# Attention: half of the outputs turned in mid-attention, outputs six items behind, and the output product begun on that half

## The chip, the core and the metric

One NeuronCore of a Trainium2 chip runs the whole program. The engines named here are TensorE (PE in the rows, its weight loads PEld), ScalarE (ACT), VectorE (DVE), GpSimd (POOL) and SyncE (SP, which issues the weight transfers). Each engine runs its own list of instructions in order, and they meet at semaphores. The metric is the device time of one execution in microseconds (us), lower is better. TensorE's clock is granted by the chip at one of two levels, 2.4 GHz (shown as 1.00) or 1.2 GHz (0.50).

## The reference, cut to what matters

256 tokens of width 1024 go through two stacks of two layers. Five attentions lie in them. In order: `x0` (cross attention of the first layer, 4 heads of 256), `dsa` (sparse attention on a shared latent, 8 heads of 128), `x1` (as `x0`), `mla` (16 heads: 8 causal latent and 8 dilated ones, 64 wide at the output) and `swa` (16 heads of 64, window and sinks). Each is scores, softmax, probabilities times values, and then a product with an output matrix that is added to the residual `h`:

```
def memory_cross_attn(h, mem_n, wq, wkv, wo):
    ...
    logits = jnp.einsum('bshd,bmhd->bhsm', q, k).astype(jnp.float32) * X_HEAD_DIM ** -0.5
    p = softmax32(logits, h.dtype)
    o = jnp.einsum('bhsm,bmhd->bshd', p, v).reshape(B_, S_, D_MODEL)
    return o @ wo
...
        h = h + memory_cross_attn(rmsnorm(h, xattn_norm[l]), mem_n, xattn_wq[l], xattn_wkv[l], xattn_wo[l])
        h = h + peer_ffn(rmsnorm(h, peer_norm[l]), peer_wq[l], peer_keys[l], peer_u[l], peer_v[l])
```

Behind every such product stands an RMS norm of `h`, which needs all of `h`. In `dsa` the heads' outputs first go through a per-head matrix `w_uv` (the groups `yc`), are put beside the output of a recurrent mixer, and then go through `odd_w_out`.

## The kernel before

**Numbers in halves.** All large products are made in three matmuls on rounded halves: left high by right high, high by low, low by high (`product`, L719 to L721). So every operand is split: ScalarE copies the high half (`wH` for weights at L495, `att_OTH` for attention outputs at L1201), and VectorE subtracts it to get the low half (`wL` at L505, `att_OTL` at L1577).

**Groups and banks.** TensorE's work is a fixed list of groups, written by `plan_groups`; each group fills one of the 8 PSUM banks, in turn, and has a reader, `act`, `dve` or `both` (ScalarE makes the high half from the bank, then VectorE the low one). A bank is used again only when its reader is done.

**Weights.** They come as a stream of blocks of 128 x 1024, two to a transfer, into `ring`; each block is split into one of 4 buffers (`NBUF`). Block b may be split once the group that reads block b - 4 last is done. Both splitting engines do this inside their own lists: `feed(eng, n)` is called ahead of each wait for group n, and puts there the splits of those blocks whose buffer is freed by a group ahead of n. So in an output product the split of block m + 4 stands in both lists between the residual adds of groups m and m + 1.

**An attention** (`attention`, in the program of each engine) walks over items, an item being a head and a half of the tokens (n = 8 items in `x0` and `x1`, 16 in `dsa`, 32 in `mla` and `swa`). At step i TensorE makes the scores S(i) (L803), turns the probabilities of item i - 2 (L816, `ATT_LAG_PT`), and multiplies those of item i - 5 with the values (L825, `ATT_LAG_O`). ScalarE makes the exponentials (L1255, L1261) and copies turned probabilities (L1270); VectorE makes maxima or logits (L1632, L1639, L1645) and scales the outputs into `att_O` (L1655, L1657). Ahead of the first turned item TensorE runs `spin`, matmuls without use.

When the last output is in `att_O`, TensorE turns `att_O` in 16 transposes into four banks (L834; token half `tt` by feature half `half`), ScalarE and VectorE make `att_OTH` and `att_OTL`, and TensorE waits for the last of these.

**The output product** (`lin`) is 8 groups, one for each 128 output features, each of 8 k by 3 matmuls. VectorE adds each group to `h` (`add`, L1613), ScalarE squares the sum for the norm (L1221), VectorE gathers squares (L1607). The norm's matmuls with ones are L740 and L742. `lin` has a second form, with `first`: then the first three groups (`LEAD`) go side by side, k by k, and `first(k)` waits for what k needs. It is used before where the input comes from a norm.

## Time and profile before

| | us |
|---|---|
| runs shown, median (lowest to highest) | 3050.76 (3049.41 to 3052.95) |
| the profiled execution, its own time | 3044.76 |
| its span, from the first to the last instruction | 3042.9 |
| TensorE matmuls busy | 2833.2 (93%) |
| VectorE busy | 1969.1 (65%) |
| ScalarE busy | 1463.9 (48%) |
| mean granted clock of TensorE | 0.964 |

The span is 1.9 us shorter than the profiled execution's own time, and that is 6.0 us below the median of the runs. Busy shares are means over stages of different kinds. An idle time in a timeline row stands in brackets at its end, with the engine and the instruction that ended it.

### The profile page before, as it was taken

The numbers are of one execution on the slowest core, as the hardware profiler recorded it, in microseconds if no ns is written. First come the engines' busy times: TensorE is split into PE (matmuls) and PEld (weight loads), VectorE is DVE, ScalarE is ACT, GpSimd is POOL, SyncE is SP. The second block draws the span as 40 slices with busy tenths as digits, with TensorE's granted clock in tenths as the row PEclk, the third lists the DMA queues.
The fourth block names the chain that finished last, engine by engine and source line by source line (L and its number), as shares of the span: only waits on it lengthen the run. The fifth ranks groups of instructions, "written<-read, shape, count | busy, mean of one in ns | idle before, by whom it ended". The sixth has DMA issues, their size and how long they took to land.

```text
span 3042.9 us, 57274 instructions
## 1 busy us (share of the span) xinstructions
PE 2833.2 (93%) x19570; PEld 2641.4 (87%) x19570; DVE 1969.1 (65%) x4218; ACT 1463.9 (48%) x2414; POOL 345.1 (11%) x199
## 2 busy tenths in 40 slices
PE   7889889999999998878899999999999789999998
PEld 6878789999988887868898999988888679998998
DVE  5544961887466666685589688557776566555555
ACT  4444344444455554454444444445555454445443
POOL 0002686000000000000069200000000000000000
PEclk8999999999999998889999999999999899999999
DMA  3434455445666664323245554666666324551454
GB/s 151 166 139 144 158 189 207 173 172 173 232 243 241 240 241 170 134 84 139 111 170 193 187 173 175 211 242 241 241 241 231 132 84 156 187 225 70 165 182 166
DMA packets 140449, 546.16 MB, mean 179 GB/s; under 512 B 15784, under 2 KB 81592, under 8 KB 83616
## 3 DMA queue, kind: packets, MB, share of 16 engines
q1 hardware_dynamic: 63216, 455.38, 41.7%
q10 hardware_dynamic: 73728, 67.14, 6.9%
q0 software_dynamic: 3376, 21.88, 1.9%
q8 instruction: 85, 1.39, 0.2%
q14 instruction: 44, 0.36, 0.0%
HBM read 505.53 MB, written 40.91 MB: 180 GB/s over the span
## 4 chain that ended last, share of the span: by engine, by line
PE 75%; DVE 8%; DMA 6%; POOL 4%; ACT 4%; issue 3%; ACTq 0%; SPq 0%; DVEq 0%
PE bank L719 22%; PE bank L720 21%; PE bank L721 21%; POOL wL L505 4%; PE bank L907 4%; DMA ring<-in_w_stream 3%; ACT wH L495 3%; DMA act_parked<-act_out 3%; DVE wL L505 2%; PE bank L803 1%; PE bank L825 1%; PE bank L816 1%; DVE act_out L1589 1%; PE bank L790 1%; DVE h L1613 1%
## 5 line engine op out<-in xcount | busy, mean ns | idle before, releaser
L505 DVE TENSOR_TENSOR wL<-ring,wH 128x1024 fp32r<-128x1024 f32 x744 | 909.2, 1225 | 769.9 <-ACT wH L495 769.1
L719 PE MATMUL bank<-hnH,wH 128*128 128x256 f32 x3648 | 1062.3, 291 | 60.8 <-DVE hnL L1571 31.0
L495 ACT ACTIVATE wH<-ring 128x1024 fp32r<-128x1024 f32 x864 | 909.3, 1055 | 341.8 <-DMA ring<-in_w_stream 160.9
L720 PE MATMUL bank<-hnL,wH 128*128 128x256 f32 x3648 | 1044.5, 286 | 0.0
L721 PE MATMUL bank<-hnH,wL 128*128 128x256 f32 x3648 | 1043.9, 286 | 0.0
L719 PEld LDWEIGHTS bank<-hnH,wH 128*128 128x128 f32 x3648 | 712.6, 195 | 72.3 <-issue 43.8
L720 PEld LDWEIGHTS bank<-hnL,wH 128*128 128x128 f32 x3648 | 713.3, 196 | 0.1
L721 PEld LDWEIGHTS bank<-hnH,wL 128*128 128x128 f32 x3648 | 711.8, 195 | 0.0
L719 PE MATMUL bank<-wH,wgtH 128*128 128x512 f32 x1024 | 399.4, 390 | 4.6 <-issue 4.5
L720 PE MATMUL bank<-wL,wgtH 128*128 128x512 f32 x1024 | 398.9, 390 | 0.0
L721 PE MATMUL bank<-wH,wgtL 128*128 128x512 f32 x1024 | 398.8, 389 | 0.0
L505 POOL TENSOR_TENSOR wL<-ring,wH 128x1024 fp32r<-128x1024 f32 x120 | 315.5, 2649 | 123.0 <-ACT wH L495 97.3
L1321 ACT ACTIVATE act_out<-bank 128x256 f32<-128x256 f32 x256 | 97.8, 382 | 393.9 <-PE bank L721 333.7
L719 PEld LDWEIGHTS bank<-wH,wgtH 128*128 128x128 f32 x1024 | 192.6, 188 | 45.4 <-issue 5.4
L1345 ACT ACTIVATE wgtH<-gates 128x256 fp32r (+1 forms) x256 | 107.0, 418 | 256.3 <-PE bank L721 255.9
L721 PEld LDWEIGHTS bank<-wH,wgtL 128*128 128x128 f32 x1024 | 192.5, 188 | 40.1
L720 PEld LDWEIGHTS bank<-wL,wgtH 128*128 128x128 f32 x1024 | 192.6, 188 | 39.9
L1741 DVE TENSOR_SCALAR onehot<-con,slotT 128x128 f32<-128x128 f32 x512 | 174.1, 340 | 0.0
L1740 DVE TENSOR_SCALAR onehot<-con,slotT 128x128 f32<-128x128 f32 x512 | 143.2, 280 | 18.7 <-ACT slotT L1360 18.7
L907 PE MATMUL bank<-onehot 128*128 128x128 f32 x1024 | 136.9, 277 | 9.1 <-DVE onehot L1741 9.1
L907 PEld LDWEIGHTS bank<-onehot 128*128 128x128 f32 x1024 | 127.0, 193 | 9.5 <-DVE onehot L1741 9.5
L1754 DVE TENSOR_TENSOR wgtL<-gates,wgtH 128x256 fp32r<-128x256 f32 x256 | 107.5, 420 | 12.8 <-ACT wgtH L1345 12.3
(347 smaller groups left out, 3398.3 us busy)
## 6 DMA issues: line engine op xcount, KB each, us to landing
ring<-in_w_stream SPq DMA_DIRECT2D x432, 1024.0 KB, 4.9
act_parked<-act_out ACTq DMA_DIRECT2D x256, 128.0 KB, 3.6
act_in<-act_parked ACTq DMA_DIRECT2D x256, 128.0 KB, 2.7
sw_bias<-in_c_swa POOLq DMA_DIRECT2D x1, 4096.0 KB, 14.6
relb_rows<-rel_table POOLq DMA_DIRECT2D x1, 2048.0 KB, 9.3
h_parked<-h POOLq DMA_DIRECT2D x2, 1024.0 KB, 6.3
h_back<-h_parked POOLq DMA_DIRECT2D x2, 1024.0 KB, 6.3
od_relb<-relb_rows POOLq DMA_DIRECT2D x2, 1024.0 KB, 8.1
```

Source lines behind the costliest of these rows:

```text
L495: eng.activation(wH[:, b % NBUF, :], raw(b), ACT.Copy).then_inc(w_high, 1)
L505: eng.tensor_tensor(wL[:, b % NBUF, :], raw(b), wH[:, b % NBUF, :].bitcast(F32), ALU.subtract).then_inc(w_low, 1)
L719: pe.matmul(dst, lh, rh, start=start, stop=False, skip_group_check=True)
L720: pe.matmul(dst, lh, rl, start=False, stop=False, skip_group_check=True)
L721: return pe.matmul(dst, ll, rh, start=False, stop=stop, skip_group_check=True)
L790: pe.matmul(psum[bank_of[n]][:, :], wH[:, b % NBUF, 0:P], wH[:, b % NBUF, 0:512], start=True, stop=True)
L907: last = pe.matmul(psacc[j][:, m * P:(m + 1) * P], onehot[:, k, :], onehot[:, 8 + k, :], start=True, stop=True)
L1321: act.activation(act_out[:, c % 2, :], psum[c % BANKS][:, 0:T], ACT.Gelu_apprx_tanh).then_inc(u_read, 1)
L1345: act.activation(wgtH[:, c % 2, :].unsqueeze(1), gates[:, bass.ds(i * 4 + c, 1), :], ACT.Copy).then_inc(wgt_high, 1)
L1740: dve.tensor_scalar(onehot[:, k, :], iota, slotT[:, 2, bass.ds(tok, 1)], None, ALU.is_equal)
L1741: last = dve.tensor_scalar(onehot[:, 8 + k, :], iota, slotT[:, 1, bass.ds(tok, 1)], slotT[:, 0, bass.ds(tok, 1)], ALU.is_equal, ALU.mult)
L1754: dve.tensor_tensor(wgtL[:, c % 2, :].unsqueeze(1), gates[:, bass.ds(i * 4 + c, 1), :], wgtH[:, c % 2, :].bitcast(F32).unsqueeze(1), ALU.s ...
```

## The change

Four things are changed, for all five attentions.

1. The lags are 3 (turned probabilities) and 6 (outputs), in place of 2 and 5, on all engines.
2. The four turned banks are no longer made at the end. Feature half 0 (two banks, 8 transposes) is turned behind step n/2 - 1 + 8, two steps after the last item of the first half of the heads has its output; half 1 at the end. ScalarE and VectorE make the halves at the same places of their lists.
3. The output products `x0o`, `x1o`, `e_out` and `o_out` use the form with three groups side by side; k = 0 waits for half 0, k = 4 for half 1.
4. In `dsa`, `yc` 0 and 1 wait for half 0 only, `yc` 2 and 3 for half 1; `odd_out` has three groups side by side, takes k = 4 to 7 first (the recurrent mixer's output), then k = 0 to 3, each behind its `yc`.

```
-ATT_LAG_PT, ATT_LAG_O = 2, 5
+ATT_LAG_PT, ATT_LAG_O = 3, 6
+ATT_LAG_OT = ATT_LAG_O + 2
...
+            def turned(kind):
+                return lambda k: read_of(pe, (kind, "OT", NT - 1, k // 4)) if k % 4 == 0 else None
...
-            def lin(name, ms, src, nk=DC, per=1, width=P, rows=T, first=None):
+            def lin(name, ms, src, nk=DC, per=1, width=P, rows=T, first=None, parts=None):
...
+                parts = list(parts or range(nk))
...
-                for k in range(nk if lead else 0):
+                for k in parts if lead else []:
...
+                def turn_outputs(half, j):
+                    read_of(pe, (kind, "O", j))
+                    for tt in range(NT):
+                        ps = bank((kind, "OT", tt, half))
+                        for c in range(4):
+                            cc = half * 4 + c
+                            last = pe.transpose(ps[:, c * P:(c + 1) * P], att_O[:, tt, cc * P:(cc + 1) * P], ident)
+                        last.then_inc(group_done, 1)
...
+                    if i - ATT_LAG_OT == len(items) // 2 - 1:
+                        turn_outputs(0, len(items) // 2 - 1)
+                turn_outputs(1, len(items) - 1)
...
-                read_of(pe, (x, "OT", NT - 1, 1))
-                lin(x + "o", range(8), (att_OTH, att_OTL))
+                lin(x + "o", range(8), (att_OTH, att_OTL), first=turned(x))
...
-            read_of(pe, ("dsa", "OT", NT - 1, 1))
             for j in range(4):
                 ps = bank(("yc", j))
+                if j % 2 == 0:
+                    read_of(pe, ("dsa", "OT", NT - 1, j // 2))
...
-            read_of(pe, ("yc", 3))
             pe.wait_ge(hg_y, 4)
-            lin("odd_out", range(8), (od_yH, od_yL))
+            lin("odd_out", range(8), (od_yH, od_yL), first=lambda k: read_of(pe, ("yc", k)) if k < 4 else None,
+                parts=(4, 5, 6, 7, 0, 1, 2, 3))
...
+                def halves_of(half):
+                    for tt in range(NT):
+                        high_of((kind, "OT", tt, half), att_OTH[:, half * 4:half * 4 + 4, tt * P:(tt + 1) * P],
+                                src=lambda ps: ps[:, :].rearrange("p (a b) -> p a b", a=4))
...
+                    if i - ATT_LAG_OT == len(items) // 2 - 1:
+                        halves_of(0)
+                halves_of(1)
```

VectorE has the same `halves_of` with `low_of`, and `e_out` and `o_out` are called as `x0o` is.

**TensorE at the end of `x0`.** Before, the last outputs (`att_PT` by `x_v`) and then the transposes of `att_O`:

```order
L825 MATMUL bank2<-x_v,att_PT 128x256 [waits read_by_act]
L825 MATMUL bank2<-x_v,att_PT 128x256
L825 MATMUL bank3<-x_v,att_PT 128x256 [waits read_by_act]
L825 MATMUL bank3<-x_v,att_PT 128x256
L834 MATMUL bank4<-con,att_O 128x128 [waits read_by_dve]
L834 MATMUL bank4<-con,att_O 128x128 x3
L834 MATMUL bank5<-con,att_O 128x128 [waits read_by_act]
L834 MATMUL bank5<-con,att_O 128x128 x3
L834 MATMUL bank6<-con,att_O 128x128 [waits read_by_dve]
```

The same place after:

```order
L844 MATMUL bank1<-x_v,att_PT 128x256 [waits read_by_act]
L844 MATMUL bank1<-x_v,att_PT 128x256
L812 MATMUL bank2<-con,att_O 128x128 [waits read_by_dve]
L812 MATMUL bank2<-con,att_O 128x128 x3
L812 MATMUL bank3<-con,att_O 128x128 [waits read_by_act]
L812 MATMUL bank3<-con,att_O 128x128 x3
L844 MATMUL bank4<-x_v,att_PT 128x256 [waits read_by_act,read_by_dve]
L844 MATMUL bank4<-x_v,att_PT 128x256
L844 MATMUL bank5<-x_v,att_PT 128x256 [waits read_by_act]
L844 MATMUL bank5<-x_v,att_PT 128x256
L812 MATMUL bank6<-con,att_O 128x128 [waits read_by_dve]
L812 MATMUL bank6<-con,att_O 128x128 x3
```

Half of the transposes now stand two outputs ahead of the end.

**TensorE at the start of `x0o`**, before and then after:

```order
L719 MATMUL bank<-att_OTH,wH 128x256 [waits w_low,read_by_dve]
L720 MATMUL bank<-att_OTL,wH 128x256
L721 MATMUL bank<-att_OTH,wL 128x256
L719 MATMUL bank<-att_OTH,wH 128x256
L720 MATMUL bank<-att_OTL,wH 128x256
```

```order
L722 MATMUL bank0<-att_OTH,wH 128x256 [waits w_low,read_by_dve]
L723 MATMUL bank0<-att_OTL,wH 128x256
L724 MATMUL bank0<-att_OTH,wL 128x256
L722 MATMUL bank1<-att_OTH,wH 128x256 [waits w_low]
L723 MATMUL bank1<-att_OTL,wH 128x256
L724 MATMUL bank1<-att_OTH,wL 128x256
L722 MATMUL bank2<-att_OTH,wH 128x256 [waits w_low]
L723 MATMUL bank2<-att_OTL,wH 128x256
```

The first matmuls went one after another to one group's bank, and now go to three groups in turn.

**VectorE from the last low halves of `x0` into `x0o`**, before and then after (`h` is the residual add, `wL` the low half of a weight block):

```order
L1577 TENSOR_TENSOR att_OTL<-bank,att_OTH 128x4x128 [waits bank_high,group_done] x4
L1613 TENSOR_TENSOR h<-h,bank 128x256 [waits group_done]
L505 TENSOR_TENSOR wL<-ring,wH 128x1024 [waits w_high]
L1613 TENSOR_TENSOR h<-h,bank 128x256 [waits group_done]
L505 TENSOR_TENSOR wL<-ring,wH 128x1024 [waits w_high]
L1613 TENSOR_TENSOR h<-h,bank 128x256 [waits group_done]
```

```order
L1595 TENSOR_TENSOR att_OTL<-bank,att_OTH 128x4x128 [waits bank_high,group_done] x2
L1631 TENSOR_TENSOR h<-h,bank 128x256 [waits group_done]
L508 TENSOR_TENSOR wL<-ring,wH 128x1024 [waits w_high]
L1631 TENSOR_TENSOR h<-h,bank 128x256 [waits group_done]
L508 TENSOR_TENSOR wL<-ring,wH 128x1024 [waits w_high]
L1631 TENSOR_TENSOR h<-h,bank 128x256 [waits group_done]
```

Two of the four low halves went away from here; behind them the order is the same in both.

## Rows read from the trace of the kernel before

**Rows 1.** The page, part 4: the chain that ended last, by engine.

```profile
PE 75%; DVE 8%; DMA 6%; POOL 4%; ACT 4%; issue 3%; ACTq 0%; SPq 0%; DVEq 0%
```

**Rows 2.** Timeline, TensorE, end of `x0`: start, duration (us), instruction, [idle before].

```profile
223.96 1.97 PE L834 MATMUL bank<-con,att_O 128*128 128x128 f32 x16 [0.65 <-DVE att_O L1657]
227.89 0.53 PE L719 MATMUL bank<-att_OTH,wH 128*128 128x256 f32 x1 [1.97 <-DVE att_OTL L1577]
```

**Rows 3.** Timeline, ScalarE and VectorE, the same stretch and the first add.

```profile
224.65 1.57 ACT L1201 ACTIVATE att_OTH<-bank 128x512 fp32r<-128x512 f32 x3 [4.38 <-PE bank L834]
...
225.35 1.29 DVE L1577 TENSOR_TENSOR att_OTL<-bank,att_OTH 128x512 fp32r<-128x512 f32 x2 [1.45 <-ACT att_OTH L1201]
...
232.55 0.42 DVE L1613 TENSOR_TENSOR h<-h,bank 128x256 f32<-128x256 f32 x1 [4.71 <-PE bank L721]
```

**Rows 4.** Timeline, VectorE and ScalarE in `e_out`: adds, and a block's split.

```profile
2502.36 0.42 DVE L1613 TENSOR_TENSOR h<-h,bank 128x256 f32<-128x256 f32 x1 [3.19 <-PE bank L721]
2504.22 1.23 DVE L505 TENSOR_TENSOR wL<-ring,wH 128x1024 fp32r<-128x1024 f32 x1 [1.44 <-ACT wH L495]
2505.36 0.41 DVE L1613 TENSOR_TENSOR h<-h,bank 128x256 f32<-128x256 f32 x1
...
2523.30 0.41 DVE L1613 TENSOR_TENSOR h<-h,bank 128x256 f32<-128x256 f32 x1
...
2503.14 1.04 ACT L495 ACTIVATE wH<-ring 128x1024 fp32r<-128x1024 f32 x1
```

**Rows 5.** Timeline, TensorE from the end of `mla` through `e_out` to the norm.

```profile
2495.30 1.97 PE L834 MATMUL bank<-con,att_O 128*128 128x128 f32 x16 [0.56 <-DVE att_O L1657]
2499.23 0.39 PE L719 MATMUL bank<-att_OTH,wH 128*128 128x256 f32 x1 [1.97 <-DVE att_OTL L1577]
...
2521.84 0.28 PE L721 MATMUL bank<-att_OTH,wL 128*128 128x256 f32 x1
2524.20 0.67 PE L740 MATMUL bank<-sq,con 128*128 128x256 f32 x2 [2.08 <-DVE sq L1607]
2524.71 0.61 PE L742 MATMUL bank<-sq,con 128*128 128x256 f32 x2
```

**Rows 6.** Timeline, end of `swa`: the transposes and the first add of `o_out`.

```profile
2803.19 0.99 PE L834 MATMUL bank<-con,att_O 128*128 128x128 f32 x7 [0.56 <-DVE att_O L1657]
...
2811.60 0.42 DVE L1613 TENSOR_TENSOR h<-h,bank 128x256 f32<-128x256 f32 x1 [4.53 <-PE bank L721]
```

**Rows 7.** Windows: stretch, length, busy PE, PEld, DVE, ACT, POOL; clock; DMA.

```profile
228.00:231.40 3.40, 3.40 (x16) 3.40 (x17) 0.00 (x0) 0.22 (x2) 0.00 (x0) 0.50 0.00 0
...
2463.00:2495.30 32.30, 31.17 (x206) 25.11 (x204) 22.07 (x126) 22.86 (x96) 0.00 (x0) 1.00 0.02 6
...
2529.00:2535.40 6.40, 6.21 (x29) 6.24 (x30) 6.07 (x15) 3.74 (x8) 0.00 (x0) 0.50 0.01 3
```

**Rows 8.** Timeline, TensorE: the norm's passes where the clock was low.

```profile
1192.34 1.19 PE L740 MATMUL bank<-sq,con 128*128 128x256 f32 x2 [2.40 <-DVE sq L1607]
1193.33 1.06 PE L742 MATMUL bank<-sq,con 128*128 128x256 f32 x2
```

**Rows 9.** Timeline, TensorE: waits for probabilities in `mla` (two) and `swa`.

```profile
2465.43 0.30 PE L816 MATMUL bank<-con,att_P 128*128 128x128 f32 x1 [0.26 <-ACT att_P L1261]
...
2493.04 0.30 PE L816 MATMUL bank<-con,att_P 128*128 128x128 f32 x1 [0.31 <-ACT att_P L1261]
...
2800.94 0.30 PE L816 MATMUL bank<-con,att_P 128*128 128x128 f32 x1 [0.37 <-ACT att_P L1261]
```

**Rows 10.** Timeline, `dsa`: the fourth logits, the last exponential, transposes, first add.

```profile
1360.40 0.43 DVE L1639 SCALAR_TENSOR_TENSOR att_L<-bank,od_relb 128x256 f32<-128x256 f32 x1 [0.52 <-PE bank L803]
...
1374.02 0.51 ACT L1261 ACTIVATE att_P<-att_L,small 128x256 f32<-128x256 f32 x1 [0.61 <-DVE small L1645]
...
1377.28 0.33 PE L834 MATMUL bank<-con,att_O 128*128 128x128 f32 x1 [0.77 <-DVE att_O L1657]
...
1389.96 0.42 DVE L1613 TENSOR_TENSOR h<-h,bank 128x256 f32<-128x256 f32 x1
```

More of the change, by code:

```diff
@@ L116, in att @@
                 g((kind, "O", i - ATT_LAG_O), "dve")
+            if i - ATT_LAG_OT == len(items) // 2 - 1:
+                for tt in range(NT):
+                    g((kind, "OT", tt, 0), "both")
         for tt in range(NT):
-            for half in range(2):
-                g((kind, "OT", tt, half), "both")
+            g((kind, "OT", tt, 1), "both")
     def norm(name):
@@ L827, in attention @@
                         last.then_inc(group_done, 1)
-                read_of(pe, (kind, "O", len(items) - 1))
-                for tt in range(NT):
-                    for half in range(2):
-                        ps = bank((kind, "OT", tt, half))
-                        for c in range(4):
-                            cc = half * 4 + c
-                            last = pe.transpose(ps[:, c * P:(c + 1) * P], att_O[:, tt, cc * P:(cc + 1) * P], ident)
-                        last.then_inc(group_done, 1)
+                    if i - ATT_LAG_OT == len(items) // 2 - 1:
+                        turn_outputs(0, len(items) // 2 - 1)
+                turn_outputs(1, len(items) - 1)
             def keys_values(l):
@@ L1141, in _ @@
                       lambda hd, s: (ml_vA if hd < 8 else ml_vB)[:, s, (hd % 8) * 64:(hd % 8 + 1) * 64])
-            read_of(pe, ("mla", "OT", NT - 1, 1))
-            lin("e_out", range(8), (att_OTH, att_OTL))
+            lin("e_out", range(8), (att_OTH, att_OTL), first=turned("mla"))
             ffn(0)
@@ L1152, in _ @@
                       lambda hd, s: sw_v[:, s, (hd // 8) * 64:(hd // 8 + 1) * 64])
-            read_of(pe, ("swa", "OT", NT - 1, 1))
-            lin("o_out", range(8), (att_OTH, att_OTL))
+            lin("o_out", range(8), (att_OTH, att_OTL), first=turned("swa"))
             ffn(1)
@@ L1235, in attention @@
                 base = att_base[kind]
+                def halves_of(half):
+                    for tt in range(NT):
+                        high_of((kind, "OT", tt, half), att_OTH[:, half * 4:half * 4 + 4, tt * P:(tt + 1) * P],
+                                src=lambda ps: ps[:, :].rearrange("p (a b) -> p a b", a=4))
                 act.activation(small[:, 82:83], eps, ACT.Exp)
@@ L1270, in attention @@
                         act.activation(att_PT[:, j % DEEP, 0:span], ps[:, 0:span], ACT.Copy).then_inc(read_by["act"], 1)
-                for tt in range(NT):
-                    for half in range(2):
-                        high_of((kind, "OT", tt, half), att_OTH[:, half * 4:half * 4 + 4, tt * P:(tt + 1) * P],
-                                src=lambda ps: ps[:, :].rearrange("p (a b) -> p a b", a=4))
+                    if i - ATT_LAG_OT == len(items) // 2 - 1:
+                        halves_of(0)
+                halves_of(1)
             def cross(l):
@@ L1619, in attention, with halves_of @@
                 hv = ATT_V[kind]
+                def halves_of(half):
+                    for tt in range(NT):
+                        place = (FULL, slice(half * 4, half * 4 + 4), slice(tt * P, (tt + 1) * P))
+                        low_of((kind, "OT", tt, half), att_OTL[place], att_OTH[place],
+                               src=lambda ps: ps[:, :].rearrange("p (a b) -> p a b", a=4))
                 for i in range(len(items) + ATT_LAG_O):
@@ L1658, in attention @@
                                           ALU.mult).then_inc(read_by["dve"], 1)
-                for tt in range(NT):
-                    for half in range(2):
-                        place = (FULL, slice(half * 4, half * 4 + 4), slice(tt * P, (tt + 1) * P))
-                        low_of((kind, "OT", tt, half), att_OTL[place], att_OTH[place],
-                               src=lambda ps: ps[:, :].rearrange("p (a b) -> p a b", a=4))
+                    if i - ATT_LAG_OT == len(items) // 2 - 1:
+                        halves_of(0)
+                halves_of(1)
             def peer(l):
```

4 lines of the change are left out of this document (2 added, 2 removed).

## The prediction

> **What bounds the kernel now.** I read the page's chain of work that ended last first: TensorE holds 75% of it [rows 1], so an edit pays only where TensorE stands still or where it takes work off TensorE. The five attentions are short stretches, so I then read the timelines of TensorE, ScalarE and VectorE around the end of each.
>
> There is a hole there. After the last head's output TensorE waits 0.65 us for VectorE, turns the outputs in 16 transposes (1.97 us) and stands another 1.97 us until the halves are made [rows 2]. ScalarE starts on the first turned bank 0.69 us after TensorE started, VectorE 0.70 us after that, and two of VectorE's low halves take 1.29 us [rows 3]. The same 1.97 us stands ahead of `e_out` [rows 5]. This is what the change is after.
>
> What ends the stage is something else. The stage behind the hole is the output product (`x0o`, `x1o`, `e_out`, `o_out`, `odd_out`): eight groups of 24 matmuls, (2521.84 - 2499.23)/191 = 0.118 us apart, so 2.84 us a group [rows 5]. Beside it VectorE adds each group to `h`. In `e_out` the first add starts at 2502.36, the second at 2505.36, the eighth at 2523.30 [rows 4]: (2523.30 - 2502.36)/7 = 2.99 us apart, longer than a group. The rows between show a closed loop: add (2502.36), ScalarE's square of it, ScalarE's split of the next weight block (2503.14, 1.04 us), VectorE's low half of it (2504.22, 1.23 us), next add (2505.36) [rows 4]. Each engine runs its list in order, and between two adds stands one block in both lists, so after the first add the loop sets the pace, however early TensorE has its groups. TensorE ends its last product at 2521.84 and stands 2.08 us for the norm, released by VectorE, whose eighth add starts at 2523.30 [rows 4, 5]. **The end of an output product is therefore the start of its first add plus 20.94 us**, and the change is to be priced at the first add.
>
> **The change, part by part.** Let T be the start of the transposes that stand behind the last head.
>
> *The end of the attention.* Before, first add - T is 232.55 - 223.96 = 8.59 us in `x0` [rows 2, 3] (1471.34 - 1462.75, the same, in `x1`, whose rows repeat these), 2502.36 - 2495.30 = 7.06 in `mla` [rows 4, 5] and 2811.60 - 2803.19 = 8.41 in `swa` [rows 6]. The extra 1.5 us in three of them is the clock: TensorE was granted 0.50 from 228.0 to 231.4, at the start of `x0o` [rows 7], that is 1.2 GHz in place of 2.4.
>
> After, 8 transposes stand there (0.98 us) and the product begins at once, on half 0. Half 1 is ready at T + 0.69 + 0.70 + 1.29 = T + 2.68, while the first four k of three groups keep TensorE until T + 0.98 + 36 x 0.118 = T + 5.2: the 1.97 us wait is hidden. But the product now begins with three groups side by side. Group 0 no longer ends after 24 matmuls but after 66 (72 less the last two groups' three each): 66 x 0.118 = 7.79 us. The first add follows the end of its group by 2502.36 - 2499.23 - 24 x 0.118 = 0.30 us [rows 4, 5]. So first add - T becomes 0.98 + 7.79 + 0.30 = 9.07 us at full clock. That is +0.48 in `x0` and `x1`, +2.01 in `mla`, +0.66 in `swa`. The three groups that are then ready together do not help: their adds still come 2.99 us apart. The weights come in time: block 4 is ready at the second add, first add + 3.0, and group 0 freed it 0.7 us before the lead's end, so it is there 2.5 us behind the lead, while group 3 keeps TensorE 2.84 us.
>
> *Turning half 0 in mid-attention.* In `x0`, `x1`, `mla` and `swa` TensorE has next to no idle time in mid-attention (31.17 of 32.30 us busy in `mla`) [rows 7], so the moved 8 transposes cost their 0.98 us there. VectorE's two low halves (1.24 us and a wait for ScalarE) come behind the output of item n/2 + 1. In `mla` and `swa` six or more items follow and the deeper lag covers it (I take 0, at most 0.5 each). In `x0` and `x1` only two outputs follow, so the last output comes about 0.40 us later: VectorE is done with half 0 1.7 us after TensorE left the transposes, and two outputs of 0.6 us each follow, to 2.9, where before it would have been 2.5.
>
> *Lags 3 and 6.* TensorE's waits for probabilities go: 0.26 at the start and 0.31 at the end of `mla`, 0.37 at the end of `swa` [rows 9]. In `x0` and `x1` there are none to win. The counts of matmuls stay.
>
> *The sparse attention `dsa`* is bound by VectorE. The fourth item's wait goes (0.52) [rows 10], and the last output that VectorE does ahead of the last logits is one less (0.46). But half 0 now stands behind the last logits: ScalarE does a 0.51 us exponential [rows 10] and the accumulator read, a copy and the first high half (about 1.65 in all, an estimate from the durations here and in rows 3) while VectorE does one output (0.5), so it stands 1.15 us and then works 1.24. Before, its waits there were 0.54 less one output, and the sum is +1.5 us at T (1377.28) [rows 10]. From T on: half 1 at 2.7 us, 12 matmuls of `yc` 1.42, then 7.79 + 0.30, so 12.25 us against 1389.96 - 1377.28 = 12.68 [rows 10]. In sum +1.05. The wait ahead of `odd_out` is gone, and the lead eats it.
>
> *The norm behind.* TensorE now ends its product at T + 0.98 + 22.7 and gets the norm at T + 9.07 + 20.94 + 0.9: it stands 7.2 us where it stood 2.08. The norm's four passes took 1.12 us (2524.20 to 2525.32) [rows 5] and, at another place where the granted clock was at the low level, 2.05 us (1192.34 to 1194.39) [rows 8]: +0.93, taken for four; half of it for `dsa`. In sum 4.2. The product behind the norm began at clock 0.50 already [rows 7], so nothing is added there. The bounds are 0 and 4.7.
>
> **Sum.** `x0` and `x1`: 0.48 + 0.98 + 0.40 = 1.86 each. `mla`: 2.01 + 0.98 - 0.57 = 2.42. `swa`: 0.66 + 0.98 - 0.37 = 1.27. `dsa`: 1.05. Together 8.5, and 4.2 for the norms: **+12.7 us**. The profiled execution took 3044.76 us (span 3042.9), the median of the runs is 3050.76, 6.0 above it; I carry the same distance: 3044.76 + 12.7 + 6.0 = 3063.4.
>
> The trace shows the low clock at the start of `x0o` after a stretch in which TensorE stood 0.65, worked 1.97 and stood 1.97 us [rows 2, 7]. The Trainium skill, page "TensorE: Matmul & The Clock Gate", section on HAM oscillation, advises arranging work so that TensorE does not stand between bursts, since it then starts the next one at half clock; the trace agrees for this hole. By the page alone the edit closes five holes and should win. By the rows it closes them and opens longer ones at the end of the same products, ahead of the norm.
>
> **Rivals.** *The gain arrives* (the other side: faster). The adds would follow TensorE, if the loop had slack: one period under 2.84 us would do, and it is 2.99. The last add would then follow T by 0.98 + 8 x 2.84 + 0.3 = 24.0 us. Before it was 8.59 + 20.94 = 29.5 in `x0` and `x1`, 28.0 in `mla`, 29.35 in `swa`; with the other terms that is -4.1, -4.1, -3.4 and -4.8, about -5 in `dsa`: -21 us, 3029. Against it: the lists of ScalarE and VectorE at the adds are unchanged, and the period is 2.99 in all five. That the loop decides only in part, and a smaller loss or none remains, is the middle case: 3048 to 3057.
>
> *The clock falls in the lead.* If TensorE gets the low level for 3.4 us at the start of the product as it does now [rows 7], the first add comes 1.6 us later in up to five places: up to +8, 3067 to 3072. For it: a wait of some 0.6 to 1.0 us stays ahead of T. Against: the 1.97 us wait goes.
>
> *The norm stays at full clock:* 8.5 us, 3059, within the forecast's own range.
>
> *The turning doesn't hide:* half 1 would have to be later than T + 5.2; from T + 2.68 that is far, and I give it nothing.
>
> **How the numbers follow.** Forecast and norm case, 3057.5 to 3067: 0.66. Low clock in the leads, 3067 to 3072: 0.15. Middle case: 0.13, nearly all of it within 0.2%. The gain arrives: 0.06. A measurement of this kernel can tell about 0.2%, 6.1 us, from no change. Slower by more: 0.66 + 0.15 and 0.01 of the middle, 0.82; the same 0.12; faster 0.06. The range of 8 in 10 is 3055 to 3070: it leaves out the gain, most of the middle case and the top of the low-clock case.
>
> **What the profile after would show.** Right: in `e_out` the first add 9.1 us behind the last transposes' start, adds 2.99 us apart, TensorE idle some 7 us ahead of the norm and its passes near 1.0 us instead of 0.5; no wait of 1.97 us behind the transposes; no wait for probabilities in `mla` and `swa`; first add - T near 9.07 in four attentions. Wrong: adds closer than 2.84 us apart (then the gain arrives), a first add 10.5 us behind T (the low clock), or a wait of TensorE in mid-attention behind half 0 of `mla` and `swa` (then the lag of six is too small).

## The result, and the profile of the changed kernel

| | before | after |
|---|---|---|
| median of the runs, us (lowest to highest) | 3050.84 (3045.64 to 3058.17, 20 runs) | 3060.96 (3047.29 to 3077.25, 20 runs) |
| ratio, 95% interval | | 1.0035 (1.0025 to 1.0046) |
| span of the profiled execution, us | 3042.9 | 3055.2 |
| mean granted clock | 0.964 | 0.959 |

The interval lies above 1: the changed kernel is slower, by some 0.35%. The ratio is worth 0.0035 x 3050.84 = +10.7 us; the spans differ by 12.3 us. The forecast was +12.7 us, 3063.4, with slower by more than 0.2% as the likeliest sign.

The page of after, part 4, answers to [rows 1]: the chain of work is TensorE's as before.

```profile
PE 76%; DVE 7%; DMA 6%; ACT 4%; POOL 4%; issue 3%; ACTq 0%; SPq 0%; DVEq 0%
```

**The hole is gone.** TensorE's timeline of after at the end of `x0` (start, duration in us, instruction, idle before it in brackets) answers to [rows 2]: two times eight transposes, and the product's first matmul directly behind the second eight.

```profile
220.06 1.04 PE L812 MATMUL bank<-con,att_O 128*128 128x128 f32 x8
...
223.92 1.09 PE L812 MATMUL bank<-con,att_O 128*128 128x128 f32 x8 [1.09 <-DVE att_O L1683]
224.77 0.36 PE L722 MATMUL bank<-att_OTH,wH 128*128 128x256 f32 x1
```

The waits for probabilities went as well. The view of TensorE's waits in after, over the whole of `mla` (2468.0 to 2504.4), has two rows, and the waits of [rows 9] are in neither:

```profile
PE bank L798 <- ACT ml_vA L1243: 1.1, 1, 1.1
PE bank L812 <- DVE att_O L1683: 0.6, 1, 0.6
```

**And a longer wait is there.** VectorE and ScalarE in `e_out` of after, against [rows 4]. The low halves of the outputs are done at 2505.78 + 1.29 = 2507.07. Then VectorE stands 6.22 us for the end of the first group:

```profile
2505.78 1.29 DVE L1595 TENSOR_TENSOR att_OTL<-bank,att_OTH 128x512 fp32r<-128x512 f32 x2 [1.45 <-ACT att_OTH L1213]
2513.29 0.42 DVE L1631 TENSOR_TENSOR h<-h,bank 128x256 f32<-128x256 f32 x1 [6.22 <-PE bank L724]
2515.15 1.23 DVE L508 TENSOR_TENSOR wL<-ring,wH 128x1024 fp32r<-128x1024 f32 x1 [1.43 <-ACT wH L498]
2516.29 0.42 DVE L1631 TENSOR_TENSOR h<-h,bank 128x256 f32<-128x256 f32 x1
...
2534.23 0.42 DVE L1631 TENSOR_TENSOR h<-h,bank 128x256 f32<-128x256 f32 x1
...
2513.75 0.42 ACT L1233 ACTIVATE sq<-h 128x256 f32<-128x256 f32 x1 [6.06 <-DVE h L1631]
2514.07 1.04 ACT L498 ACTIVATE wH<-ring 128x1024 fp32r<-128x1024 f32 x1
```

The order add, square, high half, low half, add is as before, and the adds are (2534.23 - 2513.29)/7 = 2.99 us apart. TensorE, which had its groups early, pays behind them: 6.56 us of standing where [rows 5] have 2.08, and passes of the norm at the price of [rows 8], 1.19 + 1.06 in place of 0.67 + 0.61. Its timeline in `mla` and behind `e_out`:

```profile
2468.03 1.66 PE L798 MATMUL bank<-wH 128*128 128x512 f32 x6 [1.10 <-ACT ml_vA L1243]
...
2504.39 1.09 PE L812 MATMUL bank<-con,att_O 128*128 128x128 f32 x8 [0.56 <-DVE att_O L1683]
...
2535.12 1.19 PE L747 MATMUL bank<-sq,con 128*128 128x256 f32 x2 [6.56 <-DVE sq L1625]
2536.11 1.06 PE L749 MATMUL bank<-sq,con 128*128 128x256 f32 x2
2541.04 0.55 PE L722 MATMUL bank<-hnH,wH 128*128 128x256 f32 x1 [3.87 <-DVE hnL L1589]
```

The windows of after (stretch, length, busy time of the engines, granted clock, DMA share, GB/s) answer to [rows 7]. The first stretch is the start of `x0o`, at full clock where it was at half; the second the end of the transposes of `dsa`, still low; the third the wait and the norm behind `e_out`.

```profile
223.90:233.00 9.10, 9.08 (x78) 9.08 (x79) 1.47 (x3) 2.58 (x4) 0.00 (x0) 1.00 0.01 2
...
1383.10:1387.00 3.90, 3.88 (x20) 3.89 (x21) 1.78 (x3) 1.58 (x3) 1.10 (x2) 0.56 0.12 25
2533.80:2541.00 7.20, 2.04 (x4) 1.17 (x4) 4.34 (x8) 1.87 (x5) 0.00 (x0) 0.50 0.39 146
```

**Where the time went.** Take an attention from its first matmul without use (`spin`) to the first matmul behind the norm that follows it. In `mla` of after that is 2541.04 - 2468.03 = 73.01 us. The same two rows of before:

```profile
2458.80 1.66 PE L790 MATMUL bank<-wH 128*128 128x512 f32 x6 [1.10 <-ACT ml_vA L1231]
...
2529.19 0.55 PE L719 MATMUL bank<-hnH,wH 128*128 128x256 f32 x1 [3.87 <-DVE hnL L1571]
```

give 70.39, so +2.62. The five in the order of the program grew by 2.49 (`x0`), 2.26 (`dsa`), 2.53 (`x1`), 2.62 (`mla`) and 1.31 us (`swa`), together +11.2 of the 12.3 us. The other 1.1 us lie in stretches that the change does not touch; more on these below.

### The profile page after: what moved, and what is told of

Read it like the earlier page. It is cut to its first block, busy times and chain, and to the rows that moved or that the text cites. A ratio compares the mean times of both kernels' runs of the same rounds, so it can differ in the third digit from the quotient of the medians.

```text
span 3055.2 us, 57274 instructions
## 1 busy us (share of the span) xinstructions
PE 2836.1 (93%) x19570; PEld 2642.0 (86%) x19570; DVE 1969.1 (64%) x4218; ACT 1465.6 (48%) x2414; POOL 345.0 (11%) x199
## 4 chain that ended last, share of the span: by engine, by line
PE 76%; DVE 7%; DMA 6%; ACT 4%; POOL 4%; issue 3%; ACTq 0%; SPq 0%; DVEq 0%
PE bank L722 22%; PE bank L723 22%; PE bank L724 22%; PE bank L920 4%; POOL wL L508 4%; DMA act_parked<-act_out 3%; ACT wH L498 3%; DMA ring<-in_w_stream 2%; PE bank L822 2%; DVE wL L508 1%; PE bank L844 1%; PE bank L835 1%; DVE act_out L1607 1%; PE bank L798 1%; DVE h L1631 1%
## 5 line engine op out<-in xcount | busy, mean ns | idle before, releaser
L1778 DVE TENSOR_TENSOR wgtL<-gates,wgtH 128x256 fp32r<-128x256 f32 x256 | 107.8, 421 | 12.5 <-ACT wgtH L1363 11.9
```

Source lines behind the costliest of these rows:

```text
L1778: dve.tensor_tensor(wgtL[:, c % 2, :].unsqueeze(1), gates[:, bass.ds(i * 4 + c, 1), :], wgtH[:, c % 2, :].bitcast(F32).unsqueeze(1), ALU.s ...
```

## The experiments

In all of them T is the start of the (last) transposes behind the last head, and "the attentions" is the sum of the five stretches just defined: 320.0 us in the kernel before, 331.2 in the kernel after.

### One group at the start, in place of three

```
-            def lin(..., first=None, parts=None):
+            def lin(..., first=None, parts=None, ahead=LEAD):
...
-                lead = ms[0:LEAD] if first is not None else []
+                lead = ms[0:ahead] if first is not None else []
...
-                lin(x + "o", range(8), (att_OTH, att_OTL), first=turned(x))
+                lin(x + "o", range(8), (att_OTH, att_OTL), first=turned(x), ahead=1)
```

and `ahead=1` for the other four output products.

> The kernel after, but the five output products begin with one group on half 0 (12 matmuls, then the wait for half 1) in place of three side by side. Loop theory (end of product = first add + 20.94 us, and the lead of three delays the first add): first add at T + 2.68 + 12 x 0.118 + 0.30 = T + 4.4 us where it is T + 8.9 in the kernel after, so -4.5 us in x0, x1, mla and swa, 42 matmuls less ahead of the first add of odd_out, -5.0; together -23, and up to -4.6 more if the norms return to the full clock: 3033 to 3038 us, faster than the kernel before. Rival (the loss comes from the turning in mid-attention, the lags or the norm's clock, and the lead has no part in it): within 3 us of the kernel after, 3058 to 3064.

3043.32 us, ratio to the kernel before 0.9972 (0.9960 to 0.9985). VectorE in `e_out`, T = 2494.98:

```profile
2499.44 0.42 DVE L1631 TENSOR_TENSOR h<-h,bank 128x256 f32<-128x256 f32 x1 [1.78 <-PE bank L724]
2502.43 0.42 DVE L1631 TENSOR_TENSOR h<-h,bank 128x256 f32<-128x256 f32 x1
...
2520.38 0.41 DVE L1631 TENSOR_TENSOR h<-h,bank 128x256 f32<-128x256 f32 x1
```

The first add stands at T + 4.46 (4.40 to 4.46 in the four, 4.4 expected), the others follow 2.99 us apart, the eighth at the first + 20.94. The attentions take 306.9 us, 24.3 less than in the kernel after. So the three groups side by side are what makes the changed kernel slower: with one group the same change is a gain. The median came out 5 us above the expectation's upper end, and not in the attentions, whose 24.3 us lie within the expected 23 to 27.6.

### The plain product behind the new turning

The wait for both halves and the plain `lin` of the kernel before are put back, the rest of the change stays:

```
-                lin(x + "o", range(8), (att_OTH, att_OTL), first=turned(x))
+                read_of(pe, (x, "OT", NT - 1, 1))
+                lin(x + "o", range(8), (att_OTH, att_OTL))
```

> The kernel after, but the five output products have the form and the wait of the kernel before (both halves waited for, eight groups one after another). Turning in mid-attention and the lags stay. Loop theory: first add at T + 2.68 + 2.84 + 0.30 = T + 5.8, -3.1 us in four attentions against the kernel after, about -5 in dsa, together -17, and up to -4.6 for the norms: 3039 to 3044. It would then be faster than the kernel before, and the lead would be the whole of the loss. Rival (turning in mid-attention and the lags cost more than the shorter end gives): 3051 or more.

3045.16 us, ratio 0.9989 (0.9978 to 1.0000). The first add was at T + 5.88 in `swa`, as expected, but at T + 7.37 to 7.39 in `x0`, `x1` and `mla`: TensorE stood 1.64 us for the halves ahead of `x0o` again, and from 229.5 to 232.5 its granted clock was 0.53, as in [rows 7]. The attentions took 315.6 us. The time is 1 us above the expected 3039 to 3044, and its interval ends at 1: a gain over the kernel before is not shown, one over the kernel after (1.0035) is.

Read beside the run with the lags alone (below), it prices the turning in mid-attention. T comes 6.5 us later in the sum of the five than with the lags alone (1.3 in `x0` and `x1`, 2.2 in `dsa`, 0.9 in `mla` and `swa`), and the first add is 1.2 us nearer to T where the clock at the start of the product is the same (5.88 against 7.07 in `swa`, 7.37 against 8.59 in `x1`), about 6 us in the five. With a plain product behind it the early turning therefore brings nothing; what it makes possible is a product that begins on half 0.

### Three groups side by side alone

```
-                lin(x + "o", range(8), (att_OTH, att_OTL))
+                lin(x + "o", range(8), (att_OTH, att_OTL), first=lambda k: None)
```

and so for the other four; nothing else of the change.

> The kernel before, but the five output products have three groups side by side, after the same wait for both halves; nothing is turned early and the lags are 2 and 5. Loop theory: first add 42 matmuls later, 42 x 0.118 = 4.96 us, and the norm waits so much longer: +3.4 us (where the clock at the start of the product comes back to full) to +5.0 in each of five, +17 to +25, and +0.9 for each norm that falls to the low clock, at most 4.6: 3068 to 3080. Rival (the adds catch up with the three ready groups): the last add follows TensorE, no change, 3049 to 3053.

3084.44 us, ratio 1.0113 (1.0098 to 1.0127). VectorE in `x0o`, T = 223.91:

```profile
235.92 0.42 DVE L1613 TENSOR_TENSOR h<-h,bank 128x256 f32<-128x256 f32 x1 [8.13 <-PE bank L721]
...
256.85 0.41 DVE L1613 TENSOR_TENSOR h<-h,bank 128x256 f32<-128x256 f32 x1
```

The first add is at T + 12.01 in all four, from 1.97 + 1.97 + 7.79 + 0.30 = 12.03. Against the kernel before the first adds come 3.42 (`x0`, `x1`), 4.94 (`dsa`), 4.95 (`mla`) and 3.60 us (`swa`) later, 20.3 in sum, and with 4.3 for the norms and 0.2 ahead of T in `dsa` the attentions grew by 24.8 us to 344.8, as expected (17 to 25, and at most 4.6 for the norms). The time is 4.4 us above the expected 3068 to 3080; the two stretches that no edit touches, of which more below, were 8.8 and 8.7 us longer than in the trace of before. The rival, that the adds catch up with three finished groups, is out: (256.85 - 235.92)/7 = 2.99 us apart here too.

### Opening the loop

ScalarE makes the split ahead of its wait for the add:

```
-                        added(act, adds or order[order.index(name) - 1], c)
+                        last = adds or order[order.index(name) - 1]
+                        if ADDS.get(last) in ("x0o", "odd_out", "x1o", "e_out", "o_out"):
+                            feed(act, NO[(ADDS[last], c)] + 1)
+                        added(act, last, c)
```

> The kernel after, but in the five output products ScalarE splits the high half of the next weight block ahead of its wait for the add, not behind its square of the sum; the same instructions otherwise. Loop theory: the loop is open, the adds catch up with TensorE, the eighth follows T by 0.98 + 8 x 2.84 + 0.3 = 24.0 us in place of 29.8: -5.8 us in four, about -5 in dsa, and 0 to -4.6 for the norms: 3028 to 3033. Adds behind the first three groups 2.84 us apart, the first ones 2.1 to 2.6. Rival (the pace of 2.99 us is the engines' own work, not the order): adds stay 2.99 us apart and the time within 3 us of the kernel after.

3033.84 us, ratio 0.9950 (0.9934 to 0.9966): 27 us below the kernel after, by moving one instruction of each step in ScalarE's list. VectorE, ScalarE and, in the last row, TensorE in `x0o`, T = 226.49:

```profile
235.39 0.42 DVE L1634 TENSOR_TENSOR h<-h,bank 128x256 f32<-128x256 f32 x1 [6.22 <-PE bank L724]
237.69 0.41 DVE L1634 TENSOR_TENSOR h<-h,bank 128x256 f32<-128x256 f32 x1
239.15 0.41 DVE L1634 TENSOR_TENSOR h<-h,bank 128x256 f32<-128x256 f32 x1
...
240.95 0.42 DVE L1634 TENSOR_TENSOR h<-h,bank 128x256 f32<-128x256 f32 x1
...
245.02 1.23 DVE L508 TENSOR_TENSOR wL<-ring,wH 128x1024 fp32r<-128x1024 f32 x1 [3.32 <-ACT wH L498]
246.16 0.42 DVE L1634 TENSOR_TENSOR h<-h,bank 128x256 f32<-128x256 f32 x1
...
235.45 1.06 ACT L498 ACTIVATE wH<-ring 128x1024 fp32r<-128x1024 f32 x1 [5.67 <-PE bank L724]
...
243.93 1.06 ACT L498 ACTIVATE wH<-ring 128x1024 fp32r<-128x1024 f32 x1 [3.91 <-DMA ring<-in_w_stream]
...
254.48 1.22 PE L749 MATMUL bank<-sq,con 128*128 128x256 f32 x2 [1.34 <-ACT sq L1236]
```

The split starts at 235.45, 0.06 us behind the start of the add where it was 0.78 in the kernel after, and the adds come 2.30 and 1.46 us apart: the 2.99 us were the order and not the work. The first add is still at T + 8.91. The next limit shows at once: with the splits made this early, ScalarE waits 3.91 us for the transfer of a weight block, and the fifth add comes 5.2 us behind the fourth. The eighth add is at T + 25.1 in `x0`, late by this wait, and at T + 23.7 in `x1`, where 24.0 was expected and TensorE's last group sets it.

This edit stands at all eight groups, and it has a price of its own: at the eighth group ScalarE's square, for which the norm waits, now stands behind the split of a block that is still on its way. In `x0`, `mla` and `swa` the norm's second pair of matmuls waits 1.34, 1.18 and 1.34 us for that square, and the next product begins 7.1 to 7.2 us behind the start of the norm, in `dsa` and `x1` 5.1.

### The same edit in the kernel before

The same lines, for groups 0 to 6 only (`c < DC - 1`), so that the last square stays ahead of the split behind it.

> The kernel before, but in the five output products ScalarE splits the next weight block ahead of its wait for the add (for groups 0 to 6), as in the run of the kernel after with the same edit. Loop theory: the pitch of the adds falls from 2.99 us to TensorE's 2.84, so the eighth add comes 7 x 0.15 = 1.05 us earlier in each of five: -5 us, 3045 to 3047. With the kernel after and the same edit at 3034, the change itself would then be worth about -11 us once the loop is open. Rival (the pace is the engines' own work): 2.99 stays, 3050.

VectorE in `x0o`:

```profile
233.22 0.42 DVE L1616 TENSOR_TENSOR h<-h,bank 128x256 f32<-128x256 f32 x1 [4.71 <-PE bank L721]
...
236.04 0.42 DVE L1616 TENSOR_TENSOR h<-h,bank 128x256 f32<-128x256 f32 x1 [0.45 <-PE bank L721]
...
253.00 0.42 DVE L1616 TENSOR_TENSOR h<-h,bank 128x256 f32<-128x256 f32 x1 [0.45 <-PE bank L721]
```

Seven steps take 19.78 us, 2.83 each, and every add now waits for TensorE. The norm follows 0.94 us behind the product where it was 2.08. The attentions fell by 8.9 us to 311.1: 5.8 for the loop (20.94 to 19.78 in each of the five), most of the rest because `x1o` and `o_out` began at full clock here (first adds at T + 7.06 and 7.07, where the kernel before has 8.59 and 8.41). But the time did not fall: 3049.47 us, ratio 1.0001 (0.9991 to 1.0010), where 3045 to 3047 was expected.

**Where did 9 us go?** In the two profiled executions, into code that no kernel here edits. From the end of `x0` to `dsa` (258.9 to 1365.3) and from the end of `x1` to `mla` (1504.5 to 2470.5), the windows of before, then of this kernel:

```profile
259.40:1354.20 1094.80, 1028.55 (x6860) 952.21 (x6860) 734.88 (x1638) 524.73 (x798) 187.19 (x91) 0.96 0.54 190
1498.20:2458.80 960.60, 919.48 (x6122) 849.19 (x6122) 685.38 (x1541) 472.07 (x719) 144.66 (x56) 0.98 0.57 201
```

```profile
258.90:1365.30 1106.40, 1040.07 (x6860) 962.55 (x6860) 735.18 (x1638) 524.90 (x798) 187.08 (x91) 0.95 0.54 187
1504.50:2470.50 966.00, 924.79 (x6123) 854.68 (x6123) 686.14 (x1541) 472.64 (x719) 144.50 (x56) 0.97 0.57 200
```

The same 6860 matmuls keep TensorE busy 11.5 us longer, at a clock of 0.95 in place of 0.96, and the second stretch is 5.4 us longer. The place can be seen: some 28 and 62 us behind the end of the attention `x0`. TensorE's timeline of before has a wait of 1.00 us,

```profile
286.37 0.33 PE L719 MATMUL bank<-wH,pr_qH 128*128 128x128 f32 x1 [1.00 <-DVE pr_qL L1577]
```

and that of this kernel the same,

```profile
285.11 0.33 PE L719 MATMUL bank<-wH,pr_qH 128*128 128x128 f32 x1 [1.00 <-DVE pr_qL L1580]
```

and two windows behind it read, before and then in this kernel:

```profile
288.00:296.00 8.00, 8.00 (x71) 8.00 (x71) 0.43 (x1) 4.39 (x7) 4.50 (x2) 1.00 0.30 123
322.00:330.00 8.00, 8.00 (x69) 8.00 (x68) 7.79 (x51) 3.60 (x6) 5.84 (x4) 1.00 0.20 80
```

```profile
288.00:296.00 8.00, 8.00 (x39) 8.00 (x39) 0.00 (x0) 2.74 (x4) 1.44 (x2) 0.50 0.22 92
322.00:330.00 8.00, 8.00 (x39) 8.00 (x39) 7.79 (x50) 2.22 (x5) 0.30 (x1) 0.50 0.37 132
```

Behind the same wait of 1.00 us, and with TensorE busy for 8.00 of 8.00 us, one kernel is granted 2.4 GHz and does 71 matmuls, the other 1.2 GHz and 39. By these counts 10 us at the low level do the work of 5.5 at the high one: each such stretch costs about 4.5 us, an estimate.

The two stretches together are 16.9 us longer here, more than the 9 us that were to be explained. That is because a profile shows one execution: the one of the kernel before took 6.1 us less than the median of its runs, the one of this kernel 3.2 us more. By the ratio, which no single execution decides, the code outside the attentions takes some 9 us more in this kernel.

### Matmuls without use ahead of the norm

```
             def rms(name):
                 i = NORM_NO[name]
+                if name in ("peer0", "x1", "peer1", "ffn0", "ffn1"):
+                    spin(26)
```

> The kernel after, with 26 matmuls without use (0.21 us each at full clock, 5.5 us) on TensorE ahead of the five norms behind the output products, where it stands 6.6 us. If the low clock of the norm comes from this idle time: the passes take 1.1 us again in place of 2.05, -4 to -5 us over five, and the product behind the norm may begin at the full clock too, up to -1.7 each: 3048 to 3057. Rival (the norm's clock is not set by the idle time ahead of it): passes stay 2.05 us, 3060 to 3062.

TensorE behind `e_out`:

```profile
2545.28 0.67 PE L749 MATMUL bank<-sq,con 128*128 128x256 f32 x2 [0.47 <-DVE sq L1627]
2545.79 0.59 PE L751 MATMUL bank<-sq,con 128*128 128x256 f32 x2
```

The passes are back at 0.67 + 0.59 in all five, the next product begins 0.93 to 0.95 us earlier in four of them and the attentions are 5.3 us shorter than in the kernel after (325.9): the term of the norm is what it was taken for, the clock behind an idle TensorE. The length of the wait does not decide it by itself: in the run with one group the norm behind `e_out` came after a wait of 2.09 us and was at the low clock (1.19 + 1.06), the one behind `x0o` after 2.84 us and at the full one (0.67 + 0.59). But the kernel is not faster than the kernel after: 3066.21 us, ratio to before 1.0055 (1.0042 to 1.0067), 5 us above it and outside both the expected 3048 to 3057 and the rival's 3060 to 3062. The two untouched stretches took 1104.4 and 965.3 us. The Trainium skill, page "TensorE: Matmul & The Clock Gate", section on HAM oscillation, would have TensorE kept from standing; for the norm itself the trace agrees (its four passes take 2545.79 + 0.59 - 2545.28 = 1.10 us in place of 2.05), but the kernel as a whole got no faster by it.

### The lags alone

```
-ATT_LAG_PT, ATT_LAG_O = 2, 5
+ATT_LAG_PT, ATT_LAG_O = 3, 6
```

> The kernel before with lags 3 and 6 in place of 2 and 5, nothing else. The waits for probabilities go (0.57 us in mla, 0.37 in swa, 0.5 in dsa), nothing in x0 and x1: -1.4 us, 3048 to 3051, no difference that can be measured. Rival (the deeper lag delays the last output by one item's work): +0.3 to +0.6 in each of five, 3052 to 3053.

3048.01 us, ratio 1.0000 (0.9988 to 1.0011). T came 1.03, 0.97 and 1.11 us earlier after the first `spin` in `mla`, `swa` and `dsa` and 0.04 in `x0` and `x1`: 3.2 us, against 1.4 expected. The attentions were 7.9 us shorter (312.1). The rest of it is the clock behind T, which was full in three places where the trace of before has it low: first add at T + 6.96 in `x0` (8.59 before), T + 10.98 in `dsa` (12.68) and T + 7.07 in `swa` (8.41). The first untouched stretch was 11.2 us longer than before (1106.0).

### Both remedies together

One group at the start, and the split ahead of the wait (groups 0 to 6).

> The kernel after with one group on half 0 in place of three, and ScalarE's split of the next block ahead of its wait for the add (groups 0 to 6). First add at T + 4.4, adds 2.84 us apart, the eighth at T + 24.3 where the one-group run has 25.4: -1.05 us in each of five against that run's 3043, 3037 to 3039. Against the run with three groups and the same order (3034) it tells whether the three groups side by side still cost anything once the loop is open: by the loop theory neither form is more than 1 us per product ahead of the other. Rival (weight transfers limit the adds once the loop is open): adds further apart than 2.84 from the fifth on, 3040 or more.

**3028.15 us, ratio 0.9934 (0.9921 to 0.9946)**: 20 us faster than the kernel before and the fastest here. VectorE, then TensorE, in `x0o`, T = 225.17:

```profile
229.63 0.42 DVE L1634 TENSOR_TENSOR h<-h,bank 128x256 f32<-128x256 f32 x1 [1.77 <-PE bank L724]
...
232.45 0.42 DVE L1634 TENSOR_TENSOR h<-h,bank 128x256 f32<-128x256 f32 x1 [0.45 <-PE bank L724]
...
249.41 0.42 DVE L1634 TENSOR_TENSOR h<-h,bank 128x256 f32<-128x256 f32 x1 [0.44 <-PE bank L724]
...
250.31 0.67 PE L747 MATMUL bank<-sq,con 128*128 128x256 f32 x2 [0.94 <-DVE sq L1628]
```

First add at T + 4.46, eighth at T + 24.24 (expected 4.4 and 24.3), norm at full clock in all five. The attentions take 298.0 us, 22 less than before: the hole, the loop and the norm's wait are all cashed in. The time is 9 us below the expected 3037 to 3039. Of the 8.9 us by which the attentions are shorter than with one group alone, 6.9 are earlier eighth adds (2.4 in `dsa`, 1.1 or 1.2 in the others) and 2.0 the norms, at full clock in all five here and in three there.

Whether three groups side by side still cost anything once the loop is open, the runs do not show. The kernel with three groups took 3033.84 us against 3028.15, but its edit stood at the eighth group too, and the late square cost it some 2 us in each of three attentions. Its eighth adds come 1.1 us later in the sum of the five.

### The same kernels once more

Is the time of the untouched stretches a property of the kernel or of the execution? Four kernels were run and profiled again.

> The kernel before once more, unchanged. Question: is the time of the two long stretches that no kernel here edits (end of x0 to dsa, 1094.8 us with some 81 us at the low clock in the first trace; end of x1 to mla, 960.7 us with 43) a property of the kernel or of the execution? If of the execution: other values, anywhere from 1094 to 1107 and from 957 to 969, for the same kernel. If of the kernel: 1094 to 1096 and 960 to 962 again.

> The kernel after once more, unchanged. The five attentions as in its first trace (58.0, 65.2, 58.0, 73.0, 77.0 us from spin to next product, first add at T + 8.9, norms at the low clock). The two long stretches that no kernel here edits: near 1098.5 and 961 again if they belong to the kernel, 1094 to 1107 and 957 to 969 if they belong to the execution.

> The kernel before with the split first, once more. Its attentions were 8.9 us shorter in sum than in the kernel before and its time 1 us; the two long stretches were 11.6 and 5.3 us longer. If these belong to this kernel: 1104 to 1108 and 964 to 968 again, and a median of 3047 to 3052. If they belong to the execution: other values, and the median of all its runs stays where it is since executions of both kinds are in it.

> The kernel after with matmuls without use ahead of the norms, once more. Its attentions were 5.3 us shorter in sum than in the kernel after, its time 5 us longer, and the two long stretches 5.9 and 4.2 us longer. If a busier TensorE there costs clock later: 1103 to 1107 and 964 to 967 again. If it was this execution: values down to 1095 and 957, and the attentions as before.

The table has all kernels: the ratio to the kernel before with its interval, and from the profiled executions (first and second where there are two) the sum of the attentions and the two untouched stretches, in us. The stretches are differences of the rows that begin and end them, as shown for `mla`.

| kernel | ratio | attentions | end of `x0` to `dsa` | end of `x1` to `mla` |
|---|---|---|---|---|
| before | 1; 0.9999 (0.9985 to 1.0012) | 320.0; 318.6 | 1094.8; 1095.0 | 960.7; 963.8 |
| after | 1.0035 (1.0025 to 1.0046); 1.0034 (1.0013 to 1.0055) | 331.2; 331.1 | 1098.5; 1095.7 | 961.1; 956.9 |
| one group | 0.9972 (0.9960 to 0.9985) | 306.9 | 1094.6 | 966.5 |
| plain product | 0.9989 (0.9978 to 1.0000) | 315.6 | 1098.2 | 956.7 |
| three groups alone | 1.0113 (1.0098 to 1.0127) | 344.8 | 1103.6 | 969.4 |
| after, split first | 0.9950 (0.9934 to 0.9966) | 305.9 | 1106.8 | 957.3 |
| before, split first | 1.0001 (0.9991 to 1.0010); 1.0002 (0.9987 to 1.0016) | 311.1; 310.4 | 1106.4; 1108.1 | 966.0; 969.0 |
| after, matmuls ahead of the norm | 1.0055 (1.0042 to 1.0067); 1.0060 (1.0041 to 1.0080) | 325.9; 326.2 | 1104.4; 1108.6 | 965.3; 961.6 |
| lags alone | 1.0000 (0.9988 to 1.0011) | 312.1 | 1106.0 | 961.0 |
| one group, split first | 0.9934 (0.9921 to 0.9946) | 298.0 | 1101.9 | 957.1 |

Both have a part. Each attention repeats within 0.8 us, save one stretch of low clock at the start of `o_out` in the first trace of before, 1.35 us. In these four pairs the first untouched stretch repeats within 4.2 us (1094.8 and 1095.0, 1106.4 and 1108.1), less than it differs between kernels (14 us), so the kernel has a part in it. The second moves by 3 to 4 us between two executions of one kernel. But two executions are few: the 20 runs of the kernel after spread from 3047.29 us, at a mean granted clock of 0.963, to 3077.25 us at 0.954, and the attentions, equal within 0.2 us in its two traces, have hardly a part in that.

That the clock is what makes these stretches long or short can be worked out. Take half of the time at the low level as lost, which is nearly what 39 matmuls against 71 say. The clock records of the traces give 81 to 109 us at that level in the first stretch and 37 to 62 in the second. With half of it taken off, the second stretch is 937.0 to 939.6 us in all fourteen profiles, and the first 1049.6 to 1057.8. What in a kernel decides that the clock stays high or falls there is open: the stretch begins at nearly the same time in the kernels with 1095 us (258.6 to 261.6) and in those with 1104 to 1108 (256.3 to 263.7).

## Why the prediction was right, point by point

The mechanism, the sign and the size held. Three experiments carry that: three groups alone lengthened the attentions as reckoned, one group in place of three made the same change a gain, and with the loop open it gains too.

*The closed loop, end = first add + 20.94.* Right: 20.93 or 20.94 us in all five of after, 2.99 a step. It is no property of the engines, since moving the split ahead of the wait undoes it.

*First add at T + 9.07.* 8.90 in four attentions, the same in each: 0.17 us too high. The low clock in the lead, a rival with 0.15, did not come in four of them.

*The waits for probabilities.* Right in direction, too small: the deeper lag alone was worth 1.03 in `mla` and 0.97 in `swa`, where 0.57 and 0.37 stood in the sum. With the early transposes (by difference 0.89 and 0.88 us, 0.98 forecast) T came at the same place, 0.14 and 0.09 us earlier. That is why `mla` grew by 2.62 and `swa` by 1.31, against 3.35 and 2.20 forecast with their norms. The forecast for `swa` also leaned on one execution: the low clock at the start of `o_out`, first add at T + 8.41, is not there in the second trace of before, which has T + 7.08, and against that trace `swa` grew by 2.7 us.

*Mid-attention in `x0` and `x1`.* T moved by 1.29 and 1.28 us, forecast 1.38.

*`dsa` was mis-sized*: +2.26 us, of which 0.59 for the norm, against 1.05 and half of 0.93. T moved by 1.05 (forecast 1.5), but the first add stands 13.31 us behind it and not 12.25. There VectorE's last six outputs kept TensorE waiting 1.80 us ahead of the second eight transposes, and these took 1.69 us at the low clock, as did the start of `yc` (the window of 0.56 above). TensorE and VectorE in `dsa`:

```profile
1383.12 1.69 PE L812 MATMUL bank<-con,att_O 128*128 128x128 f32 x8 [1.80 <-DVE att_O L1683]
...
1396.43 0.42 DVE L1631 TENSOR_TENSOR h<-h,bank 128x256 f32<-128x256 f32 x1 [3.67 <-PE bank L724]
```

The second trace of the kernel with matmuls ahead of the norm, which has the same instructions here, shows what the clock costs: its second eight transposes began at 1396.18 at full clock,

```profile
1396.18 1.09 PE L814 MATMUL bank<-con,att_O 128*128 128x128 f32 x8 [1.80 <-DVE att_O L1685]
```

and its first add stood at T + 12.29, where 12.25 was forecast. (Counted from `spin`, that execution gained only 0.3 us in `dsa` apart from the norm: its mean clock ahead of T was 0.89 against 0.92, and T came 0.7 us later.) So this is the rival of the low clock, come true in the one place where the wait ahead of T was the longest, 1.0 of its up to 8 us.

*The norms.* Right: all five at the low clock, in each +0.9 us (0.59 in `dsa`), 4.3 in sum against 4.2; the wait was 6.57 us, not 7.2.

*The sum.* 11.2 us in the attentions against 12.7 (12.5 in the second pair of traces). What the prediction did not have at all is the term of the untouched stretches. It happened to be small between these two kernels (+3.7 and +0.4 in the first pair of traces, +0.7 and -6.9 in the second), but it was +11.6 and +5.3 us in the first trace of the split first in the kernel before, some 9 us in sum by its ratio, an edit of the same size in the attentions. The range of 15 us held because that term was small, which is luck: it had not been reckoned.

*Slips of arithmetic, none of which moves the forecast.* In the rival where the gain arrives, `mla` comes to 24.0 - 28.0 + 0.98 - 0.57 = -3.6 us and not -3.4, and in `dsa` 2.7 + 1.42 + 7.79 + 0.30 is 12.21, not 12.25.

*Distance from the span to the median.* Before, it was 3050.84 - 3042.9 = 7.9 us, and 5.8 us in after: near enough, though the runs of after spread over 30 us and those of before over 12.5.

## What to carry to other kernels

Ahead of hiding a wait in front of a product, measure what ends the product: if each step of the consumer goes around through the engines' lists (here add, square, split, low half), starting the producer earlier gives only what it brings the consumer's first step forward (with one group, 2.6 to 4.2 us in four of the products here), and interleaving its groups delays the first one that the consumer can take. Look first for the order inside those lists, since one moved instruction opened the loop, and let the product begin early with as few groups side by side as cover the wait: one did here. At the last step keep what the next stage waits for (here the square) ahead of an instruction that may wait for a transfer. And price a small edit by the sum of the places that it touches, then expect the measured time to miss that by some us either way where TensorE's clock rises and falls in code that the edit does not touch.

## What the runs showed of the hardware

TensorE's granted clock fell to 1.2 GHz for some 10 us at a time while TensorE was busy without a break (8.00 of 8.00 us in two windows above), in stretches of code that are the same in all kernels. Within 80 us behind the attention `x0` there are zero, one or two such stretches. The three kernels that were run twice with a change in them had the same number at the same places both times; the kernel before had none in its first trace and one in its second, where the window of 318.9 to 328.9 us reads

```profile
318.90:328.90 10.00, 10.00 (x48) 10.00 (x48) 9.72 (x62) 2.73 (x4) 2.27 (x2) 0.50 0.27 106
```

where the first trace has 1.00 for the same code (317.4 to 327.4). So the kernel alone does not decide it. Edits worth 9 us in the attentions (the split first in the kernel before) and 8 us (the lags alone) showed no gain in the time; in their profiles the two untouched stretches were longer by 16.9 and 11.5 us, with more of them at the low clock.

Keeping TensorE busy ahead of the norm gave the full clock to the norm and yet went with low stretches soon after, in both executions. Whether the one causes the other is not shown: kernels without these matmuls had them too.
